# Local attention's rotation from rows loaded with swapped halves instead of a product with a permutation

## The reference

```
def rotary(x, cos, sin):
    half = x.shape[-1] // 2
    rot = jnp.concatenate([-x[..., half:], x[..., :half]], axis=-1)
    return x * cos[:, None, :] + rot * sin[:, None, :]

q = rotary(rms_norm(q.reshape(b, s, SWA_Q_HEADS, SWA_HEAD_DIM), q_norm_w), cos, sin)
k = rotary(rms_norm(k.reshape(b, s, SWA_KV_HEADS, SWA_HEAD_DIM), k_norm_w), cos, sin)
```

## Time and profile before

| | |
|---|---|
| median of 3 runs | 2288.24 us (2286.06 to 2290.22) |
| the profiled execution | 2284.61 us, its span 2282.8 us |
| PE busy over the span | 2148.9 us (94%) |
| DVE, ACT, Pool busy | 51%, 32%, 16% |
| step 1 of the block, by DVE's L1352 | 364.23 to 401.17 us |
| step 2 | 401.17 to 433.33 us |
| step 3 | 433.33 to 454.42 us |

### The profile page before, as it was taken

The page is one execution under the profiler, slowest core; times in us unless marked ns, Lnnn a source line. Parts: engine busy times, 40 slices in busy tenths (PEclk is TensorE's granted clock), DMA queues, the critical chain, the costliest instruction groups (busy, mean ns, idle before and its releaser), DMA issues. The chain is left out here.

```text
span 2282.8 us, 33797 instructions
## 1 busy us (share of the span) xinstructions
PE 2148.9 (94%) x14354; PEld 1657.5 (73%) x14382; DVE 1161.6 (51%) x1718; ACT 728.0 (32%) x1272; POOL 369.5 (16%) x305
## 2 busy tenths in 40 slices
PE   7999987889886999999998887999999999999998
PEld 6888874667664777886864454777888878878887
DVE  6773325667665766553523666455433443442443
ACT  4223314233332343231313665353212222221221
POOL 3000003222233641030201221540000000000000
PEclk9999997899998899999998999999999999999999
DMA  6113321000004638411224001221111111112112
GB/s 209 47 47 101 93 86 67 2 2 2 2 2 162 187 115 323 169 47 56 58 63 172 1 1 72 86 83 47 42 44 54 43 41 57 52 36 59 47 33 97
DMA packets 185977, 165.83 MB, mean 73 GB/s; under 512 B 13448, under 2 KB 163804, under 8 KB 185700
## 3 DMA queue, kind: packets, MB, share of 16 engines
q1 hardware_dynamic: 179918, 144.67, 20.0%
q0 software_dynamic: 4928, 18.35, 2.0%
q10 hardware_dynamic: 982, 0.65, 0.1%
HBM read 136.92 MB, written 26.74 MB: 72 GB/s over the span
## 5 line engine op out<-in xcount | busy, mean ns | idle before, releaser
L250 PE MATMUL mix_acc<-mix_hi,w_hi 128*128 128x512 f32 x1040 | 415.5, 400 | 0.0
L252 PE MATMUL mix_acc<-mix_hi,w_lo 128*128 128x512 f32 x1040 | 410.0, 394 | 0.0
L251 PE MATMUL mix_acc<-m_lo,w_hi 128*128 128x512 f32 x1040 | 409.5, 394 | 0.0
L230 ACT ACTIVATE w_hi<-w_stage 128x1024 fp32r<-128x1024 f32 x154 | 162.6, 1056 | 476.3 <-PE mix_acc L252 255.8
L238 DVE TENSOR_TENSOR w_lo<-w_stage,w_hi 128x1024 fp32r<-128x1024 f32 x154 | 193.9, 1259 | 132.8 <-ACT w_hi L230 132.8
L3020 DVE SCALAR_TENSOR_TENSOR hidden<-mix_acc,hidden_conv,hidden 128x1023 f32<-128x1023 f32 x88 | 112.8, 1282 | 263.2 <-ACT hidden L2969 261.7
L250 PEld LDWEIGHTS mix_acc<-mix_hi,w_hi 128*128 128x128 f32 x1040 | 195.7, 188 | 52.3 <-issue 8.2
L252 PEld LDWEIGHTS mix_acc<-mix_hi,w_lo 128*128 128x128 f32 x1040 | 195.7, 188 | 45.9
L251 PEld LDWEIGHTS mix_acc<-m_lo,w_hi 128*128 128x128 f32 x1040 | 195.8, 188 | 43.3
L250 PE MATMUL acc<-h_hi,w_hi 128*128 128x512 f32 x400 | 156.8, 392 | 0.9 <-issue 0.9
L252 PE MATMUL acc<-h_hi,w_lo 128*128 128x512 f32 x400 | 155.8, 390 | 0.0
(11 more groups left out here) (351 smaller groups left out, 3753.6 us busy)
## 6 DMA issues: line engine op xcount, KB each, us to landing
w_stage<-in_w_in SPq DMA_DIRECT2D x48, 512.0 KB, 4.2
w_stage<-in_w_up SPq DMA_DIRECT2D x44, 512.0 KB, 3.6
w_stage<-in_w_out SPq DMA_DIRECT2D x32, 512.0 KB, 4.0
w_ada<-in_w_ada SPq DMA_DIRECT2D x32, 512.0 KB, 4.8
spill<-y_tok POOLq DMA_DIRECT2D x21, 512.0 KB, 5.0
m_resid<-resid_spill SPq DMA_DIRECT2D x2, 4096.0 KB, 14.6
conv_in<-in_w_ada SPq DMA_DIRECT2D x16, 512.0 KB, 5.8
conv_in<-spill SPq DMA_DIRECT2D x3, 2048.0 KB, 13.3
```

Source lines behind the costliest of these rows:

```text
L230: nc.scalar.activation(w_hi[:, slot], w_stage[:, slot], ACT.Copy).then_inc(w_hi_ready, 1)
L250: nc.tensor.matmul(acc[:, h, :], w_hi[:, slot, k, :], hi[:, k, tok], start=k == 0, stop=False)
L251: nc.tensor.matmul(acc[:, h, :], w_hi[:, slot, k, :], lo[:, k, tok], start=False, stop=False)
L252: mm = nc.tensor.matmul(acc[:, h, :], w_lo[:, slot, k, :], hi[:, k, tok], start=False, stop=k == kts - 1)
```

## The change

The product with the permutation is dropped. The raw rows of each unit are still in memory (`spill`), and they are loaded a second time with the two halves of every head exchanged, by four DMAs of 32 rows x 512 tokens each (64 KB) for a unit, into one of two places (`swapped`, where `turned_sin` lay, so the trace names it `y_tok`). Pool multiplies them with the sine, whose table now carries the sign, and DVE multiplies with `head_rs` and the weight in swapped order (`swapped_scaled`), then adds. Loads for unit u >= 2 wait on SP's queue until unit u-2 is rotated and its place is free. The weight in swapped order is one more column of the parameters.

```diff
+                def load_swapped(u):
+                    blk, h = norm_units[u]
+                    first = (SP_SWK if blk == 4 else SP_SWQ + blk) * P
+                    if u >= 2:
+                        sp.wait_ge(s_rope, u - 1)
+                    for i in range(4):
+                        src = first + (i ^ 1) * (HD // 2)
+                        sp.dma_start(swapped[i * HD // 2:(i + 1) * HD // 2, u % 2, :],
+                                     spill[src:src + HD // 2, h * HALF:(h + 1) * HALF]).then_inc(s_swap[u % 2], 16)
+                load_swapped(0)
+                load_swapped(1)
...
+                for u in range(2, NN):
+                    load_swapped(u)
...
                 def cos_part(u):
-                    pool.wait_ge(s_hturn, u + 1)
+                    pool.wait_ge(s_hn, 2 * u + 1)
...
+                def sin_part(u):
+                    blk, h = norm_units[u]
+                    if u == 0:
+                        pool.wait_ge(s_wconst, 48)
+                    pool.wait_ge(s_swap[u % 2], 64 * (u // 2 + 1))
+                    nc.gpsimd.tensor_tensor(swapped[:, u % 2, :], swapped[:, u % 2, :], sin[:, h * HALF:(h + 1) * HALF],
+                                            ALU.mult).then_inc(s_hcos, 1)
...
                         for u in (range(0, 8) if s == 1 else range(8, NN)):
                             cos_part(u)
-                        pool.wait_ge(s_hcos, 8 if s == 1 else NN)
+                            if 1 <= u < NN - 1:
+                                sin_part(u + 1)
+                        pool.wait_ge(s_hcos, sin_done(8) if s == 1 else cos_done(NN - 1))
                     if s:
                         store(s - 1)
...
-                    if u:
-                        pe.wait_ge(s_hln, u)
-                    nc.tensor.matmul(scb[:, 0, :], head_ones, head_sq[:, u % 2, :], start=True, stop=True
+                    if u >= 2:
+                        pe.wait_ge(s_hln, u - 1)
+                    nc.tensor.matmul(scb[:, u % 2, :], head_ones, head_sq[:, u % 2, :], start=True, stop=True
...
-                def turn_halves(u):
-                    nc.tensor.matmul(scb[:, 1, :], turn, qk[:, blk, h * HALF:(h + 1) * HALF], start=True,
-                                     stop=True).then_inc(s_hturn, 1)
...
+                def swapped_scaled(u):
+                    dve.wait_ge(s_hcos, sin_done(u))
+                    nc.vector.scalar_tensor_tensor(swapped[:, u % 2, :], swapped[:, u % 2, :], w, head_rs[:, u % 2, :],
+                                                   ALU.mult, ALU.mult).then_inc(s_hn, 1)
...
                 def rotate(u):
-                    dve.wait_ge(s_hturn, u + 1)
-                    nc.vector.tensor_tensor(turned_sin[:, u % 2, :], scb[:, 1, :], sin[:, tok], ALU.mult
-                                            ).then_inc(s_hsin, 1)
-                    dve.wait_ge(s_hsin, u + 1)
-                    dve.wait_ge(s_hcos, u + 1)
-                    nc.vector.tensor_tensor(qk[:, blk, tok], qk[:, blk, tok], turned_sin[:, u % 2, :], ALU.add
+                    dve.wait_ge(s_hn, 2 * u + 2)
+                    dve.wait_ge(s_hcos, cos_done(u))
+                    nc.vector.tensor_tensor(qk[:, blk, tok], qk[:, blk, tok], swapped[:, u % 2, :], ALU.add
...
-                    if 3 <= i < NN + 3:
-                        rotate(i - 3)
+                    if 2 <= i < NN + 2:
+                        swapped_scaled(i - 2)
+                        rotate(i - 2)
                     if 1 <= i < NN + 1:
                         normed(i - 1)
```

More of the change, by code:

```diff
@@ L39 @@
 NORM1_G, NORM2_G, GLA_NG, GLA_B, AQ_W, AK_W = 79, 87, 95, 96, 98, 99
-PARAM_ROWS = 100
+SQ_SWAPPED, SK_SWAPPED = 100, 101
+PARAM_ROWS = 102
 HIDDEN = 2 * D_FF // P
@@ L51, in shape_constants @@
     head_ones = (half[:, None] == half[None, :]).astype(f)
-    turn = np.zeros((P, P), f)
-    for m in range(P):
-        base, r = m // 64 * 64, m % 64
-        turn[base + (r + 32) % 64, m] = -1.0 if r < 32 else 1.0
     inv = f(10000.0) ** (-np.arange(0, HD, 2, dtype=f) / f(HD))
@@ L60, in shape_constants @@
     cos, sin = np.cos(ang).astype(f), np.sin(ang).astype(f)
+    sin = np.where((np.arange(P) % HD < HD // 2)[:, None], -sin, sin)
     t = np.arange(SEQ)
@@ L89, in shape_constants @@
         "base": {"ident": ident, "ones": ones},
-        "rope": {"head_ones": head_ones, "turn": turn, "cos": cos, "sin": sin},
+        "rope": {"head_ones": head_ones, "cos": cos, "sin": sin},
         "dn": {"reset": reset},
@@ L841, in build @@
         region = sb("window_region", [P, 18 * P], F32, stS)
-        const_sb["rope"] = region[:, 0:18 * P]
-        head_ones, turn = const("head_ones"), const("turn")
+        const_sb["rope"] = region[:, 0:17 * P]
+        head_ones = const("head_ones")
         cos, sin = const("cos"), const("sin")
@@ L874, in build @@
                                              sem("head_rs_ready"), sem("head_normed"))
-        s_hturn, s_hsin, s_hcos, s_rope, s_small = (sem("halves_turned"), sem("sin_part"), sem("cos_part"),
-                                                    sem("rotated"), sem("small_ready"))
+        s_swap = [sem("halves_loaded0"), sem("halves_loaded1")]
+        s_hcos, s_rope, s_small = sem("sin_or_cos_part"), sem("rotated"), sem("small_ready")
         s_vt, s_vc = sem("window_v_turned"), sem("window_v_copied")
@@ L883, in build, with sin_done, cos_done @@
         NA, NN = len(att_units), len(norm_units)
+        def sin_done(u):
+            return 2 * u + 1 if u >= 2 else u + 1
+        def cos_done(u):
+            return 2 * u + 2 if u else 3
         def key_tiles(i):
@@ L1001, in _ @@
                         decayed(s)
+                    if s <= 2:
+                        pool.wait_ge(s_kdec, 2 * s + 2)
+                    if s == 0:
+                        sin_part(0)
+                        sin_part(1)
+                        pool.wait_ge(s_hcos, 2)
                     if s in (1, 2):
-                        pool.wait_ge(s_kdec, 2 * s + 2)
                         for u in (range(0, 8) if s == 1 else range(8, NN)):
                             cos_part(u)
-                        pool.wait_ge(s_hcos, 8 if s == 1 else NN)
+                            if 1 <= u < NN - 1:
+                                sin_part(u + 1)
+                        pool.wait_ge(s_hcos, sin_done(8) if s == 1 else cos_done(NN - 1))
                     if s:
@@ L1279, in head_scale @@
                     if u >= 2:
-                        act.wait_ge(s_hn, u - 1)
-                    nc.scalar.activation(head_rs[:, u % 2, :], scb[:, 0, :], ACT.Ln, bias=eps[:, 0:1],
+                        act.wait_ge(s_hn, 2 * (u - 1))
+                    nc.scalar.activation(head_rs[:, u % 2, :], scb[:, u % 2, :], ACT.Ln, bias=eps[:, 0:1],
                                          scale=1.0 / HD).then_inc(s_hln, 1)
@@ L3075, in launch_arrays @@
     head = lambda a: np.concatenate([a.reshape(-1), a.reshape(-1)])[None]
+    swapped_head = lambda a: head(np.roll(a.reshape(-1), HD // 2))
     param_rows = np.concatenate([
```

27 lines of the change are left out of this document (12 added, 15 removed).

## The result

The changed kernel takes 2292.53 us (median of 18 executions; 17 of them lie between 2284.9 and 2299.8 us, and the ratio leaves out one of 2455.78 us, whose granted clock was 0.827 where theirs was 0.965 to 0.972), the kernel before in the same job 2288.18 us (18 executions, 2282.61 to 2293.59). The ratio is 1.0021 with a 95% interval of 1.0012 to 1.0030: slower by 4.35 us. The forecast was +10.1 us.

A forecast was written before the change was run, and what follows sets the result against it. The prediction took DVE's work plus its waits for PE to bound step 1, with Pool and DVE then sharing a port. Terms 5.2 + 2.4 + 2.5 = +10.1 us on 2288.24 gave 2298.3 us, range 2288.5 to 2303.

The forecast's parts named there:

- Step 1, +5.2: Step 1 of the block: DVE and Pool excluding each other at their port lengthen it by 5.2 us.
- The pace: Step 1, from one unit's rotation to the next: 4.4 us a unit, against 4.33 before.
- The second count: Step 1 summed by DVE: +2.0 us of work, +7 standing behind Pool, 3.8 less behind PE: +5.2.
- The reading that 9.0 us behind PE fill the 9.2 us of idle time: Step 1 before the change: DVE's waits for PE, 9.0 us, make up nearly all its 9.2 us not busy.
- the standing still: Steps with Pool products: a DVE instruction with two SBUF inputs halts until Pool's ends, then needs its last 0.56 us.
- the rival of 16 in 100: Steps 1 and 2: DVE does not halt behind these Pool products; no measurable change, 2287 to 2291.5 us; 16 in 100.
- Step 2 up to its first mask, +2.4: First half of step 2: `rotate(8)` waits for Pool's `cos_part(8)`, delaying the mask PE needs by 2.4 us.
- The clock, +2.5: Mainly second half of step 2: less busy PE falls to 1.2 GHz, costing 2.5 us, bounds -2.3 to +6.2.
- the shift found: Whole kernel: steps 1 and 2 lengthen by 10.1 us, carried unchanged to the end and added to the median 2288.24.
- PE's relief: Step 1: ten dropped products cut DVE's waits behind PE by some 3.8 us; as deciding rival -6.8 us, 7 in 100.
- SP, DMAs, ACT: nothing: Steps 0 to 2: the added loads stay hidden and ACT gets no work, cost nothing; late-loads rival 2311 us, 6 in 100.

The follow-up runs named there:

- no_sine: Changed kernel without Pool's ten sine products, loads and DVE's work kept, output lacking the sine factor: 2287.34 us, ratio 0.9998 to the kernel before.
- early_interleaved: Changed kernel with 8 large early loads behind the constants, two DVE operations a unit, Pool's sine products two units ahead between cosine products: 2282.78 us, ratio 0.9985 to before.
- pool_order: Changed kernel with Pool's last three products moved ahead of v_scaled(2) and decayed(2): 2288.10 us, ratio 1.0007 to the kernel before.
- before_b: Kernel before, unchanged, profiled a second time: 2283.76 us, steps 1 and 2 together 72.9 us.
- before_c: Kernel before, unchanged, profiled a third time: 2283.19 us, steps 1 and 2 together 68.9 us.
- dummy: Changed kernel with an unread PE product at each place of the permutation's, head sums back to one bank: 2297.91 us, ratio 1.0055 to the kernel before.
- early_sine: Changed kernel with large early loads ahead of the last constants, all ten sine products in step 0, two DVE operations a unit: 2291.14 us, ratio 1.0019 to before.

## Why the prediction was right in kind and too large in size

**Step 1, +5.2: right mechanism, a little low in the profiles.** Measured +6.9 in the profiled pair, and 42.1 to 44.0 against 36.7 to 37.9 us over all. `rotate(0)` was forecast 8.8 us behind the step's start and came at 8.9 (375.25 - 366.33). The pace was taken as 4.4 us a unit and is (407.83 - 375.25) / 7 = 4.65: seven times 0.25 is the 1.7 us that was missing. The second count holds in its total, less in its parts: DVE's work was to grow by 2.0 + 7 and grew by 9.65; its waits behind PE were to shrink by 3.8 and shrank by 5.4 (8.2 to 2.8 us inside the step), and 2.9 us behind Pool came in, which this count had at nothing. The reading that 9.0 us behind PE fill the 9.2 us of idle time counted 2.08 us of step 0; inside the step it is 8.2, and 1.0 is ACT's wait and hand-overs. no_sine shows the cause: without Pool's second product the step is at 37.1 us again. The forecast had read the standing still from three rows of before, and it held with Pool's full-height products too, so the rival of 16 in 100 is out as a mechanism, though its upper end (2291.5 us) lies as near the result as the forecast's lower one. The Trainium skill has this as an exclusive lock between the two engines ("SBUF — State Buffer", the section on who interferes with whom); by its rule the change would be slower, which is the sign that came, and the rows agree with an exclusion: in early_interleaved it works in both directions (1.64 us for 0.75 on DVE, 1.71 for 1.26 on Pool).

**Step 2 up to its first mask, +2.4: right.** +2.8 (13.66 against 10.8 us), with a wait of 5.67 us where 5.5 was forecast. pool_order takes this wait away.

**The clock, +2.5: right in the profiles.** In the profiled pair the second half of step 2 grew by 6.27 - 2.8 = 3.5 us. Over eleven profiled executions step 2 as a whole went from 33.7 to 38.4 us in the mean, +4.7, where 2.4 + 2.5 = 4.9 was forecast. The clock was to be under 0.8 in both steps and was 0.71 and 0.64. The pair's step 2 of before is one of the shorter ones (32.1 to 36.3 us, before_b the longest), which explains 1.5 us of the pair's difference but not the median: by its granted clock over the whole program, 0.974, that execution is typical of before, whose 35 timed executions in the second job have 0.973 in the mean.

**The step that failed: the shift found in two steps was carried whole to the kernel's end and added to the median.** The prediction says that "the shift found is added to the median", and that steps from 3 on are unchanged, so that the shift reaches the end of the kernel. It put everything behind step 2, and the difference between a profiled and a timed execution, at nothing. Measured are +10.9 us in steps 1 and 2, for 10.1, but +4.35 and +4.71 us in the medians of the whole kernels (4.3 and 5.6 in means, standard errors 1.1 and 1.0). So 5.4 to 5.8 us of the forecast are missing, outside the terms that were costed. Three things are known of them.

First, the length of these two steps does not fix the kernel's time. early_interleaved is 5.3 us longer than before in them and 2.9 us faster; before_b is 4.0 us longer than before_c and ends 0.6 us later; dummy is as long as the changed kernel and 6.5 us slower. With ten products put back on PE (and the second bank taken away), a shift of this size does reach the end (+11.0 us); without them it does not. The prediction looked for what PE's relief is worth in step 1 alone.

Second, the profiled executions of the changed kernel are slow ones: 2299.79 us is the slowest of 17, 2296.38 of 12, 760.64 of the 4 cut ones, and the first has a granted clock of 0.965 where its 17 have 0.969 in the mean. The five whole profiles of before, 2283.2 to 2285.9 us, lie at or under the low end of that kernel's medians of three executions and more (2285.65 to 2288.24), though its cut profile is the slowest of five as well. No record shows the steps of a timed execution that was not profiled, so the +10.9 us may themselves be smaller there; at the block's end timed executions have 6.6 to 7.9.

Third, where profiles give something back, it is behind the block, and it is little: the same code takes 1583.1 to 1587.7 us in five executions of before and 1577.7 to 1584.1 in four of the changed kernel, 3.3 less in the mean with a standard error of 1.8, while steps 3 to the last scores take 2.4 more. What brings the timed kernels down to +4.4 us therefore stays open. One place can be pointed at. Here is the stretch from 190 to 205 us behind the block's last scores, in before, the changed kernel and dummy:

```profile
885.10:900.10 15.00, 14.12 (x64) 11.46 (x63) 9.82 (x8) 1.97 (x2) 3.28 (x4) 0.89 1.05 402
```

```profile
904.00:919.00 15.00, 15.00 (x76) 12.67 (x75) 8.26 (x6) 2.18 (x3) 3.28 (x4) 1.00 1.05 400
```

```profile
897.80:912.80 15.00, 13.97 (x63) 11.40 (x62) 9.72 (x8) 1.97 (x2) 3.27 (x4) 0.89 1.05 401
```

A fall of the clock lies there in all five profiles of before and in dummy, and in none of the other kernels. So what PE did in the block goes with what its clock does 200 us later, and dummy, with the products put back, behaves like before. What makes it so is open, and this fall alone is small: PE is busy 14.12 of 15 us with it and 15.00 without.

**SP, DMAs, ACT: nothing, right.** The 64 KB loads land 2.0 us after their issue, near the 2.4 taken. Pool's sine products did wait for them in step 1, 8.0 us in six waits of at most 2.5, with 0.6 us of it passed on to DVE. Part of the pace's missing 0.25 us may lie here; it was not separated from the port, since no_sine removes both. Step 3 takes 21.09 us, as in before and as forecast.

**PE's relief.** In step 1 it was taken as 3.8 us and is 5.4 inside the step. Over timed executions the ten products may be worth more: dummy, which puts them back, is some 6.5 us slower than the changed kernel. How much of that belongs to the bank that dummy takes away, and in which stretch it lies, was not separated.

## What to carry to other kernels

Before moving work from PE to Pool, count for each unit the time that Pool and DVE hold their shared port, not each engine's busy share: here the change was to fill 4.2 us of a 4.3 us pace, while Pool read as 39% busy before it. The pace became 4.65 us. Where PE's clock changes, a shift that is read from profiles of a stretch is not yet a shift of the median: here the two steps grew by 10.9 us and the kernel by 4.4. Compare whole timed executions, and kernels cut behind the block with enough of them, before the shift is carried to the end. Before large loads are moved ahead, the small ones that share a semaphore with an early use belong in front of them.

## What was not expected of the hardware

- The exclusion works in both directions: with Pool never idle its product is stretched from 1.26 to 1.71 us, while DVE's is from 0.75 to 1.64 (early_interleaved). In the changed kernel, too, one Pool product took 1.71 us.
- An execution's time goes with its mean granted clock within one kernel. Of 35 executions of the kernel before in one job, from 2280.8 to 2292.6 us, with clocks from 0.977 to 0.969, the correlation is -0.92. Between kernels it doesn't hold: dummy has a mean clock of 0.970 and a mean time of 2298.4 us, the changed kernel 0.968 and 2292.0 (second job).
- A small load takes the time of what stands ahead of it on SP's queue: 96 KB issued last landed after 20.6 us (early_sine), and after 7.2 us when issued ahead of the large loads (early_interleaved).
